# First modulation tiles regrouped by chunk, with the first norm's chunks finished pair by pair

## The chip, the cores and the metric

The kernel runs on one core of a Trainium2 chip. The metric is the device time of one execution in microseconds (us); lower is better. PE is TensorE (matrix multiply), PEld its weight loads, DVE is VectorE, ACT is ScalarE, POOL is GpSimd, SP is the engine whose queue issues most DMAs.

## The reference, cut to what matters

Two layers of a hybrid block (retention, neighbourhood attention and grouped attention, gated and merged) run on 256 latent and 256 context tokens of width 1024, followed by feed-forward and mixer stages. All is float32. At the head stands an adaptive norm; for layer 0:

```python
shift_x, scale_x, gate_x = jnp.split((c_silu @ ada_w + ada_b)[:, None, :], 3, axis=-1)
shift_y, scale_y, gate_y = jnp.split(cc_silu @ ada_w + ada_b, 3, axis=-1)
hx = rms_norm(x, norm_w) * (1.0 + scale_x) + shift_x
hy = rms_norm(y, norm_w) * (1.0 + scale_y) + shift_y
... = split_cols(hx @ w_in)
```

`ada_w` is 1024 x 3072 per layer, so scale and shift of layer 0 take 2048 of its columns, 8 MB. Everything that comes after needs hx and hy.

## The kernel before, in words

Activations lie transposed: 8 chunks of 128 features on the partitions, 512 token columns (256 latent, 256 context). Weights come as tiles of 128 x 1024 floats (512 KB), in the order of `TILES`, through a ring of 6 buffers `raw` that SP's queue refills as PE releases them (L1140 to L1154). A float32 product is made of three matmuls on rounded halves: each weight tile is split by ACT (`w_hi`, L1361) and DVE (`w_lo`, L1641), each activation chunk into `h_hi` and `h_lo`; `three` (L2117) multiplies them (L2121 to L2123). A product has 8 chunks of three matmuls, 24 in all.

The order of work is a list of steps that `build_schedule` writes (L695); every engine walks through the same list and runs its own part of each step in that order, with semaphore waits. An engine that waits in one step does nothing of the later ones.

The head before: SP loads half of the tokens and then the weight tiles; ACT's queue loads the parameters, the other half of the tokens and the tables `con` (610 KB, L1321). The first 16 tiles are the modulation weights of layer 0: eight of scale, then eight of shift (`ADA_FIRST`). One tile holds 128 of the 1024 input rows and all 1024 columns of its section, so a section is known only when its eighth tile is in. PE multiplies each tile by silu(c) with 32 columns of the array and 512 moving columns (L2168, two strips of 32 a tile; neighbouring tiles use the other two strips). After a section ACT copies the bank to `merge_tanh` (L1348), PE turns it (L2182), DVE adds the bias (L1681, L1683). Beside this ACT squares the tokens (L1371), DVE sums (L1654), PE takes means (`norm_mean`, L2211), DVE adds epsilon (L1714), POOL takes the power (L1220), PE spreads it (L2220) and DVE copies it to `rstd` (L1706). When scale is known DVE computes `m` = x * a * rstd for all chunks (L1668, 16 instructions of 256 columns). When shift is known ACT writes `h_hi` = m + shift (L1399) and DVE `h_lo` = m + shift - h_hi (L1777), chunk by chunk, with three weight splits between (at chunks 0, 3 and 6), and PE starts the first product. POOL loads and completes two bias tables beside it (L1176, L1181). Layer 1's norm (L1664, L1396, L1405, L1772) has the same work in another form: DVE x * rstd in one instruction, ACT scale and shift in place and a copy to `h_hi`, DVE the difference.

Of the kernel before, what the change touches and what calls it, by code (L numbers as in the profile page):

```python
# [54 lines left out]
ADA_FIRST = [(0, 1), (0, 0)]  # L55
# [5 lines left out]
def tile_order():  # L61

    out = [("ada", layer, section, k) for layer, section in ADA_FIRST for k in range(KC)]
# [120 lines left out]
def lay_out_params(a):  # L184
# [24 lines left out]
def shape_tables():  # L209
# [16 lines left out]

        "window": np.where((kc >= start) & (kc < start + 16), 0.0, -1e30),
# [49 lines left out]
class Schedule:  # L277


    def __init__(self):  # L280
# [4 lines left out]
        self.split_n = AHEAD  # L285
# [33 lines left out]
    def split_ahead(self, t):  # L319

        done = t - sum(tile[0] == "ada" for tile in TILES[:t])
# [34 lines left out]
    def product(self, what, src, n, blocks=KC, parts=(3, 3, 2), **fields):  # L356
# [10 lines left out]
        at = 0  # L367
        for part in (parts if blocks == KC else (2, 2)):
# [245 lines left out]
def ada_tile(s, section, k):  # L614
# [3 lines left out]
    if section not in ADA_FIRST:  # L618
        s.flush()
        s.split_ahead(s.tile)  # L620
# [60 lines left out]
def normed(s, norm, k):  # L681
# [3 lines left out]
    if split:  # L685
        st.at = s.count("shift") if norm.layer else None
# [8 lines left out]
def build_schedule():  # L695
# [4 lines left out]
    for k in range(KC):  # L700
        ada_tile(s, ADA_FIRST[0], k)
        if k == 3:
            norm_mean(s, norm)
        if k == 5:
            norm_spread(s, norm)
    for k in range(KC):
        ada_tile(s, ADA_FIRST[1], k)
        if k == 1:
            s.turn_due()
            s.add("ada_scale", layer=0)  # L710
            for i in range(KC):
                prescale(s, norm, i)
    s.turn_due()
    for layer in range(DEPTH):
        norm.how, norm.layer = "ada", layer
        if layer:
            s.add("ada_scale", layer=layer)
            rms(s, norm)
        for k in range(KC):
            if layer:  # L720
                for i in range(3 * k if k < 1 else k + 2, min(k + 3, KC)):
                    prescale(s, norm, i)
            elif k in (0, 3, 6):
                s.add("split", t=SPLIT_TILES[(0, 3, 6).index(k)])
            normed(s, norm, k)
# [125 lines left out]
def block_kernel(nc, weights, params, consts, tokens, rpb, gate_a, gate_x, spatial, spatial_b, out):  # L851
# [4 lines left out]
    with ctx:  # L856
# [44 lines left out]

        o_hi = {"a": hb("oa_hi", [P, 4, BOTH], F32R)}
# [25 lines left out]

        hb("reserved", [P, 8 * BOTH + 4 * BOTH + 2 * BOTH + BOTH + 4 * BOTH + 12 * P])
        half_tanh, head_sq = scaled[:, 0, :], scaled[:, 1, :]  # L930
        merge_tanh = hb("merge_tanh", [P, 2, BOTH])

        ada_rows = [merge_tanh[:, 0, :], bias[:, :, :, :].rearrange("p a b c -> p (a b c)")[:, 0:BOTH]]
        work = hb("work", [P, 4, BOTH])
        probs, probs_t = work[:, 0:2, :], work[:, 2:4, :]
        abs_dif = hb("abs_dif", [P, 3 * P])
# [57 lines left out]
        con_landed = sem("con_landed")  # L994
        tok_landed = [sem(f"tok_landed{i}") for i in range(4)]
        c_zero = sem("c_zero")
        ada_part = sem("ada_part")
        prescaled = sem("prescaled")
        shifted = sem("shifted")
# [89 lines left out]
        def rows_of(u):  # L1089
            return ada_rows[0 if (u.layer, u.c) in ADA_FIRST + [ADA_LAST] else 1]  # L1090

        def adds_on_dve(st):
            return st.norm.n == 0

# [41 lines left out]
        shift_turn = {st.u.layer: st.u for st in steps if st.kind == "ada_turn" and st.u.c == 0}  # L1136
# [26 lines left out]
        def _(pool):  # L1163
# [6 lines left out]
            def bias_step(st):  # L1170
# [3 lines left out]
                if reader[slot] is not None:  # L1174
                    pool.wait_ge(biased, reader[slot] + 1)
                pool.dma_start(bias[:, slot, :, :], rpb[g.layer, g.c]).then_inc(bias_landed[slot], 16)  # L1176
# [1310 lines left out]
```

## Time and profile before

| | us |
|---|---|
| median of 3 runs | 2096.53 (2094.64 to 2099.82) |
| the profiled execution | 2094.94 |
| its span, first to last instruction | 2093.0 |
| PE busy | 1993.6 (95%) |
| DVE busy | 1116.9 (53%) |
| ACT busy | 894.7 (43%) |
| POOL busy | 257.8 (12%) |

The span is cut into 40 slices of 52.3 us in the page; the whole head that the change touches lies in the first. In a timeline a row gives the start, the length, the engine, the line, what is written and read, how many instructions are merged, and in brackets the idle time before and what ended it.

### The profile page before, as it was taken

Reading aid. Unit: us, or ns where it says so; the run is one execution under the profiler, and the core shown is the slowest. Engines: PE = TensorE matmul, PEld = TensorE weight load, DVE = VectorE, ACT = ScalarE, POOL = GpSimd, SP = SyncE. Lnnn points to the kernel's source line nnn. Section 1 sums busy time; section 2 is a strip of 40 time slices with the busy share of each in tenths; the row PEclk is TensorE's granted clock in tenths of the full one; section 3 lists DMA queues with packets and bytes.
Section 4 is the critical chain, followed back from the end, with each engine's and each line's share of the span. In section 5 each row is a group of like instructions: output and inputs, shape, how many; then the busy total and the mean of one; then the engine's idle time right before and its main releaser. Section 6 shows DMA issues by size and latency. Waiting matters only on the chain.

```text
span 2093.0 us, 36804 instructions
## 1 busy us (share of the span) xinstructions
PE 1993.6 (95%) x13960; PEld 1782.5 (85%) x13960; DVE 1116.9 (53%) x1776; ACT 894.7 (43%) x1441; POOL 257.8 (12%) x278
## 2 busy tenths in 40 slices
PE   6999999999999999999989999899999999899998
PEld 3777777777786788888989998889999999899997
DVE  5454442455433664545565556865555555575554
ACT  4444231344332544335444444654444444554443
POOL 1000110110112101101131001400001000200001
PEclk9999999999999899999989999989999999899998
DMA  7221444311225223333445554445555555345552
GB/s 301 78 69 61 141 141 137 115 61 61 77 94 169 88 97 95 108 132 101 141 136 177 182 184 144 143 129 183 181 184 166 181 183 186 123 142 180 181 182 89
DMA packets 78970, 289.06 MB, mean 138 GB/s; under 512 B 8848, under 2 KB 8976, under 8 KB 78864
## 3 DMA queue, kind: packets, MB, share of 16 engines
q1 hardware_dynamic: 77168, 281.05, 40.6%
q0 software_dynamic: 1120, 4.72, 0.7%
q8 instruction: 76, 1.25, 0.2%
q10 hardware_dynamic: 576, 1.80, 0.2%
q14 instruction: 30, 0.25, 0.1%
HBM read 286.49 MB, written 1.05 MB: 137 GB/s over the span
## 4 chain that ended last, share of the span: by engine, by line
PE 59%; DVE 4%; issue 2%; ACT 2%; POOL 1%; POOLq 0%; DVEq 0%; ACTq 0%
PE bank L2121 18%; PE bank L2123 18%; PE bank L2122 18%; PE bank L2211 1%; ACT w_hi L1361 1%; PE bank L2290 1%; PE bank L2273 1%; DVE w_lo L1641 1%; PE bank L2259 1%; DVE h_lo L1721 1%; PE bank L2220 0%; PE bank L2330 0%; DVE x L2020 0%; DVE r_conv L2054 0%; PE bank L2315 0%
## 5 line engine op out<-in xcount | busy, mean ns | idle before, releaser
L2121 PE MATMUL bank<-h_hi,w_hi 128*128 128x256 f32 (+1 forms) x2720 | 874.5, 322 | 30.6 <-DVE h_lo L1721 12.6
L2123 PE MATMUL bank<-h_hi,w_lo 128*128 128x256 f32 (+1 forms) x2720 | 851.2, 313 | 0.0
L2122 PE MATMUL bank<-h_lo,w_hi 128*128 128x256 f32 (+1 forms) x2720 | 850.2, 313 | 0.0
L1641 DVE TENSOR_TENSOR w_lo<-raw,w_hi 128x1024 fp32r<-128x1024 f32 x484 | 597.2, 1236 | 415.8 <-ACT w_hi L1361 415.1
L1361 ACT ACTIVATE w_hi<-raw 128x1024 fp32r<-128x1024 f32 x484 | 509.8, 1055 | 524.9 <-PE bank L2123 467.1
L2121 PEld LDWEIGHTS bank<-h_hi,w_hi 128*128 128x128 f32 x2720 | 522.8, 192 | 93.8 <-issue 52.3
L2123 PEld LDWEIGHTS bank<-h_hi,w_lo 128*128 128x128 f32 x2720 | 522.9, 192 | 28.8
L2122 PEld LDWEIGHTS bank<-h_lo,w_hi 128*128 128x128 f32 x2720 | 523.9, 193 | 23.0
L2121 PE MATMUL bank<-hid_hi,w_hi 128*128 128x256 f32 x704 | 197.8, 281 | 1.8 <-DVE hid_lo L1982 1.8
L2123 PE MATMUL bank<-hid_hi,w_lo 128*128 128x256 f32 x704 | 197.6, 281 | 0.0
L2122 PE MATMUL bank<-hid_lo,w_hi 128*128 128x256 f32 x704 | 197.2, 280 | 0.0
L1255 POOL TENSOR_TENSOR silu_g<-silu_g,rstd 128x256 f32<-128x256 f32 x88 | 65.3, 743 | 659.3 <-ACT silu_g L1520 659.3
L2121 PEld LDWEIGHTS bank<-hid_hi,w_hi 128*128 128x128 f32 x704 | 132.9, 189 | 2.4 <-DVE w_lo L1641 2.4
L2122 PEld LDWEIGHTS bank<-hid_lo,w_hi 128*128 128x128 f32 x704 | 132.8, 189 | 0.0
L2123 PEld LDWEIGHTS bank<-hid_hi,w_lo 128*128 128x128 f32 x704 | 132.4, 188 | 0.0
L1520 ACT ACTIVATE silu_g<-silu_g 128x256 f32<-128x256 f32 x88 | 36.8, 418 | 163.0 <-DVE silu_g L1967 163.0
L1976 DVE TENSOR_TENSOR hidden<-silu_g,bank 128x256 f32<-128x256 f32 x88 | 37.0, 421 | 129.0 <-POOL silu_g L1255 126.5
L1458 ACT ACTIVATE work<-bank,row_stat 128x512 f32<-128x512 f32 (+1 forms) x96 | 58.3, 612 | 68.3 <-DVE row_stat L1862 68.3
L1468 ACT ACTIVATE work<-bank 128x512 f32<-128x512 f32 (+1 forms) x96 | 45.3, 525 | 78.8 <-PE bank L2273 78.6
L1862 DVE TENSOR_REDUCE row_stat<-bank 128x1 f32<-128x512 f32 (+1 forms) x96 | 53.1, 594 | 33.7 <-PE bank L2259 33.5
L1242 POOL TENSOR_TENSOR scaled<-scaled,square 128x512 f32<-128x512 f32 (+1 forms) x32 | 44.1, 1378 | 184.5 <-ACT square L1371 183.9
L1215 POOL TENSOR_TENSOR m<-m,square 128x512 f32<-128x512 f32 (+1 forms) x32 | 33.3, 1043 | 218.8 <-DVE square L1808 218.8
(223 smaller groups left out, 2142.1 us busy)
## 6 DMA issues: line engine op xcount, KB each, us to landing
raw<-in_weights SPq DMA_DIRECT2D x532, 512.0 KB, 3.3
bias<-in_rpb POOLq DMA_DIRECT2D x8, 384.0 KB, 3.6
x<-in_tokens SPq DMA_DIRECT2D x2, 512.0 KB, 6.1
x<-in_tokens ACTq DMA_DIRECT2D x2, 512.0 KB, 8.5
out<-rows_out SPq DMA_DIRECT2D x1, 1024.0 KB, 4.0
con<-in_consts ACTq DMA_DIRECT2D x1, 609.5 KB, 11.8
ws<-in_spatial POOLq DMA_DIRECT2D x1, 512.0 KB, 4.9
ws_b<-in_spatial_b POOLq DMA_DIRECT2D x1, 512.0 KB, 5.6
```

The source lines that it names most:

```text
L1242: pool.tensor_tensor(sum_sq[:, 0:n], sum_sq[:, 0:n], square_of(st), ALU.add).then_inc(sq_added, 1)
L1255: pool.tensor_tensor(v, v, rstd[:, 0:SEQ], ALU.mult).then_inc(silu_scaled, 1)
L1361: nc.scalar.activation(w_hi[:, n % SPLIT, :], raw[:, t % RAW, :], ACT.Copy).then_inc(hi_ready, 1)
L1458: nc.scalar.activation(probs[:, hp, 0:u.keys], S[use % 2][:, 0:u.keys], ACT.Exp, bias=row_stat[:, 0, i:i + 1], accum_out=row_stat[:, 1, i: ...
L1468: nc.scalar.activation(probs_t[:, hp, 0:u.keys], T[use % 2][:, 0:u.keys], ACT.Copy)\
L1520: nc.scalar.activation(silu_g[:, i % 2, :], silu_g[:, i % 2, :], ACT.Silu).then_inc(silu_ready, 1)
L1641: dve.tensor_tensor(w_lo[:, t % RAW, :], raw[:, t % RAW, :], w_hi[:, SPLIT_NO[t] % SPLIT, :].bitcast(F32), ALU.subtract).then_inc(lo_ready, 1)
L1862: dve.tensor_reduce(row_stat[:, 0, i:i + 1], s[:, 0:u.keys], AX_X, ALU.max, negate=True)\
L1976: dve.tensor_tensor(hidden[:, i % 2, :], silu_g[:, i % 2, :], S[i % 2][:, 0:SEQ], ALU.mult)\
L2121: nc.tensor.matmul(dst, w_hi[:, SPLIT_NO[t] % SPLIT, at], hi, start=start, stop=False, skip_group_check=shared)
L2122: nc.tensor.matmul(dst, w_hi[:, SPLIT_NO[t] % SPLIT, at], lo, start=False, stop=False, skip_group_check=shared)
L2123: return nc.tensor.matmul(dst, w_lo[:, t % RAW, at], hi, start=False, stop=stop, skip_group_check=shared)
```

## The change: what it does

- The 16 first tiles leave the ring and come from an array of their own, `first`: tile 2k is the shift columns and 2k+1 the scale columns of chunk k, with all 1024 rows. They land in buffers that are used only later (`early`, `early_o`, `work`), so none of them waits for another. SP issues all 16, with the first weight tile after pair 4, then five ring tiles, then the rest of the tables; ACT's queue loads only the first 133 table columns.
- For each pair PE makes 16 multiplications of 128 columns over four strips, ACT copies 256 columns, PE sums the strips with `parts` (two calls of two moving columns each), DVE adds the bias and makes `ada_a`. PE waits for ACT's copy inside the step.
- The first norm is done as in layer 1: x * rstd in one instruction (chunks 0 to 3 on DVE, 4 to 7 on POOL), then per chunk: even ones ACT (scale and shift in place, then a copy), odd ones ACT straight into `h_hi` and DVE the full value into `scaled`; DVE the difference.
- Steps now run: pairs 0 to 2, mean, pair 3, spread, the eight x * rstd, chunks 0 to 3, pair 4, chunk 4, pair 5, chunk 5, first weight split, pair 6, chunk 6, first two chunks of the first product, pair 7, chunk 7, three more splits, the rest of the product. POOL's first bias load waits for pair 7 to have landed.

```diff
-ADA_FIRST = [(0, 1), (0, 0)]
+def lay_out_first(a):
+    tiles = [column_tile(a["ada_w"][0], slice(D * c + P * k, D * c + P * k + P)) for k in range(KC) for c in range(2)]
+    return np.stack(tiles)
...
-CONSTS = [("ident", P), ("swap", P), ("cos", SEQ), ("sin", SEQ),
-          ("dif", 3 * P), ("window", GRID_W), ("ones", 1),
-          ("heads", 2)]
+CONSTS = [("ident", P), ("ones", 1), ("heads", 2), ("parts", 2),
+          ("swap", P), ("cos", SEQ), ("sin", SEQ), ("dif", 3 * P), ("window", GRID_W)]
+EARLY = P + 5
...
+        if self.hold:
+            parts = (2, 3, 3)
...
+    for k in range(KC - 1):
+        pair(k)
+        if k == 2:
+            norm_mean(s, norm)
         if k == 3:
-            norm_mean(s, norm)
-        if k == 5:
             norm_spread(s, norm)
...
             for i in range(KC):
                 prescale(s, norm, i)
-    s.turn_due()
+            for i in range(k + 1):
+                normed(s, norm, i)
+        if k > 3:
+            normed(s, norm, k)
+        if k == 5:
+            s.add("split", t=SPLIT_TILES[0])
+
+    def last_pair():
+        pair(KC - 1)
+        normed(s, norm, KC - 1)
+        s.hold = False
+        s.split_ahead(0)
+
+    s.background = [last_pair]
...
-            for t in range(RAW):
+            for k in range(KC):
+                for c in range(2):
+                    sp.dma_start(first_tiles[2 * k + c], first[2 * k + c, :, :]).then_inc(first_landed[k], 16)
+                if k == 4:
+                    sp.dma_start(raw[:, 0, :], weights[0, :, :]).then_inc(raw_landed[0], 16)
+            for t in range(1, RAW):
                 sp.dma_start(raw[:, t, :], weights[t, :, :]).then_inc(raw_landed[t], 16)
+            sp.dma_start(con[:, EARLY:], consts[:, EARLY:]).then_inc(tab_landed, 16)
...
+            def prescale_step(st):
+
+                if st.norm.layer or st.k < 4:
+                    return
+                pool.wait_ge(m_free, st.norm.m_spread + 1)
+                pool.tensor_tensor(m[:, st.k, :], x[:, st.k, :], rstd[:, :], ALU.mult).then_inc(pool_scaled, 1)
...
+            def ada_pair_step(st):
+
+                act.wait_ge(t_full, st.t_use + 1)
+                nc.scalar.activation(pair_rows[:, st.k % 2, :], T[st.t_use % 2][:, 0:SEQ], ACT.Copy)\
+                    .then_inc(t_free[st.t_use % 2], 1)
...
+                    ins = nc.scalar.activation((m if st.how == "act" else h_hi)[:, k, at], m[:, k, at], ACT.Identity,
+                                               bias=ada[:, norm.layer, k, j:j + 1], scale=ada_a[:, k, j:j + 1])
...
+            def ada_pair_step(st):
+
+                k = st.k
+                dve.wait_ge(m_full, st.m + 1)
...
+                dve.tensor_tensor(dst, M[:, 0:4].rearrange("p (c j) -> p c j", c=2), b, ALU.add).then_inc(m_free, 1)
+                dve.wait_ge(m_free, st.m + 1)
+                dve.scalar_tensor_tensor(out=ada_a[:, k, :], in0=ada[:, 0, KC + k, :], scalar=1.0,
+                                         in1=par[:, nw:nw + 1].to_broadcast([P, 2]), op0=ALU.add, op1=ALU.mult)\
+                    .then_inc(a_ready, 1)
...
+                if st.how == "dve":
+                    full = scaled[:, st.at % 2, :]
+                    dve.wait_ge(*scaled_by_norm(norm, k))
+                    dve.wait_ge(a_ready, k + 1)
+                    for j in range(2):
+                        at = slice(SEQ * j, SEQ * j + SEQ)
+                        ins = dve.tensor_scalar(full[:, at], m[:, k, at], ada_a[:, k, j:j + 1], ada[:, 0, k, j:j + 1],
+                                                ALU.mult, ALU.add)
+                    ins.then_inc(shift_dve, 1)
+                    dve.wait_ge(shift_dve, st.at + 1)
                 dve.wait_ge(h_hi_ready, st.h + 1)
+                dve.tensor_tensor(h_lo[:, k, :], full, h_hi[:, k, :].bitcast(F32), ALU.subtract)\
+                    .then_inc(h_lo_ready, 1)
...
+            def ada_pair_step(st):
+
+                k, use = st.k, st.t_use
+                if k == 0:
+                    pe.wait_ge(set_up_act, 2)
+                pe.wait_ge(first_landed[k], 32)
+                if use >= 2:
+                    pe.wait_ge(t_free[use % 2], use // 2)
+                for c in range(2):
+                    for i in range(KC):
+                        strip = 32 * (i % 4)
+                        ins = nc.tensor.matmul(T[use % 2][strip:strip + 32, P * c:P * c + P], c_silu[:, i, :],
+                                               first_tiles[2 * k + c][:, P * i:P * i + P], start=(i < 4), stop=(i >= 4),
+                                               skip_group_check=True)
+                ins.then_inc(t_full, 1)
...
+                pe.wait_ge(*t_out(use))
+                if st.m:
+                    pe.wait_ge(m_free, st.m)
+                for c in range(2):
+                    ins = nc.tensor.matmul(M[:, 2 * c:2 * c + 2], pair_rows[:, k % 2, P * c:P * c + P], C_("parts"),
+                                           start=True, stop=True)
+                ins.then_inc(m_full, 1)
```

## Rows read from the trace of the kernel before

**Rows 1.** Stages; columns: length, busy PE, PEld, DVE, ACT, POOL, PEclk, DMA, GB/s
```profile
11.00:17.30 6.30, 5.49 (x14) 0.78 (x16) 4.15 (x6) 3.67 (x6) 0.00 (x0) 1.00 1.02 411
...
37.80:44.60 6.80, 5.25 (x12) 4.12 (x13) 6.80 (x14) 6.80 (x15) 0.72 (x1) 0.50 0.39 155
```

**Rows 2.** Timeline of PE in the head, modulation tiles and norm
```profile
11.07 1.92 PE L2168 MATMUL bank<-raw,c_silu 128*32 128x512 f32 x4 [11.07 <-DMA raw<-in_weights]
...
19.72 1.07 PE L2168 MATMUL bank<-raw,c_silu 128*32 128x512 f32 x8
21.21 1.16 PE L2220 MATMUL bank<-con,stats 128*128 128x128 f32 x8 [0.42 <-POOL stats L1220]
...
32.80 1.05 PE L2168 MATMUL bank<-raw,c_silu 128*32 128x512 f32 x4 [0.24 <-DMA raw<-in_weights]
```

**Rows 3.** Timeline of all engines, from the squares to rstd
```profile
15.00 0.63 ACT L1371 ACTIVATE square<-x 128x512 f32<-128x512 f32 x1 [0.17 <-DVE scaled L1654]
...
17.84 0.38 PE L2211 MATMUL bank<-con,scaled 128*128 128x1 f32 x2
...
19.83 0.16 DVE L1714 TENSOR_SCALAR stats<-bank 128x4 f32<-128x4 f32 x1 [4.12 <-PE bank L2211]
20.14 1.02 POOL L1220 TENSOR_TENSOR stats<-stats,neg_half 128x4 f32<-128x4 f32 x1 [18.93 <-DVE stats L1714]
...
22.40 0.69 DVE L1706 COPY rstd<-bank 128x512 f32<-128x512 f32 x1 [2.42 <-PE bank L2220]
```

**Rows 4.** Timeline of all engines, from the last modulation tile to the first matmuls
```profile
34.64 0.65 PE L2182 MATMUL bank<-con,merge_tanh 128*128 128x128 f32 x4 [0.78 <-ACT merge_tanh L1348]
...
36.58 1.94 POOL L1181 TENSOR_TENSOR bias<-bias,con 128x768 f32<-128x768 f32 x1 [6.50 <-DMA bias<-in_rpb]
...
39.35 0.76 PE L2121 MATMUL bank<-h_hi,w_hi 128*128 128x512 f32 x1 [4.06 <-DVE h_lo L1777]
...
40.77 0.63 PE L2121 MATMUL bank<-h_hi,w_hi 128*128 128x512 f32 x1
...
42.05 0.63 PE L2121 MATMUL bank<-h_hi,w_hi 128*128 128x512 f32 x1
```

**Rows 5.** Timeline of PE, the first matmuls of the second product
```profile
47.87 0.39 PE L2121 MATMUL bank<-h_hi,w_hi 128*128 128x512 f32 x1
...
48.56 0.39 PE L2121 MATMUL bank<-h_hi,w_hi 128*128 128x512 f32 x1
```

**Rows 6.** One line each, min/median/max ns: L1777 around 37 us, then L1664
```profile
L1777 DVE SCALAR_TENSOR_TENSOR h_lo<-m,ada,h_hi x1: 2034/2034/2034, 36.8 to 36.8; 128x256 fp32r<-128x256 f32 x1
...
L1664 DVE TENSOR_TENSOR m<-x,rstd x8: 677/678/2300, 679.4 to 689.9; 128x512 f32<-128x512 f32 x8
```

**Rows 7.** Groups by shape, whole span: busy us, mean ns, idle before
```profile
L1641 DVE TENSOR_TENSOR w_lo<-raw,w_hi 128x1024 fp32r<-128x1024 f32 x484 | 597.2, 1236 | 415.8 <-ACT w_hi L1361 415.1
...
L1361 ACT ACTIVATE w_hi<-raw 128x1024 fp32r<-128x1024 f32 x484 | 509.8, 1055 | 524.9 <-PE bank L2123 467.1 <-DMA raw<-in_weights 57.4
...
L1215 POOL TENSOR_TENSOR m<-m,square 128x512 f32<-128x512 f32 x16 | 20.6, 1289 | 145.8 <-DVE square L1808 145.8
...
L1876 DVE TENSOR_SCALAR work<-work,row_stat 128x256 f32<-128x256 f32 x32 | 10.7, 376 | 0.0
...
L1399 ACT ACTIVATE h_hi<-m,ada 128x256 fp32r<-128x256 f32 x16 | 6.7, 494 | 0.3 <-DVE ada L1683 0.3
L1405 ACT ACTIVATE h_hi<-m 128x512 fp32r<-128x512 f32 x8 | 5.0, 630 | 0.3
...
L1598 ACT ACTIVATE sg_vt<-bank 128x256 f32<-128x256 f32 x8 | 3.0, 371 | 5.2 <-PE bank L2440 5.2
```

**Rows 8.** Timeline of ACT in layer 1's norm: scale and shift in place
```profile
683.48 1.08 ACT L1396 ACTIVATE m<-m,ada,ada_a 128x256 f32<-128x256 f32 x2
```

**Rows 9.** Timeline of PE, narrow matmuls on two strips of 64 columns
```profile
76.18 1.09 PE L2290 MATMUL bank<-work,v_s 128*64 128x128 f32 x16
```

More of the change, by code:

```diff
@@ L61, in tile_order @@
 def tile_order():
-    out = [("ada", layer, section, k) for layer, section in ADA_FIRST for k in range(KC)]
+    out = []
     for layer in range(DEPTH):
@@ L617, in ada_tile @@
         s.section = Step("section", s.count("section"), layer=section[0], c=section[1], t_use=s.use("T"))
-    if section not in ADA_FIRST:
-        s.flush()
-        s.split_ahead(s.tile)
+    s.flush()
+    s.split_ahead(s.tile)
     s.add("ada_tile", tile=s.tile, u=s.section, k=k)
@@ L685, in normed @@
     if split:
-        st.at = s.count("shift") if norm.layer else None
+        st.how = "act" if norm.layer or k % 2 == 0 else "dve"
+        st.at = s.count("shift_" + st.how)
     norm.chunks.append(st)
@@ L848, in ffn_tile, with block_kernel @@
     return (0 if i == 0 else 3 * i - 1) + (which == "u")
-def block_kernel(nc, weights, params, consts, tokens, rpb, gate_a, gate_x, spatial, spatial_b, out):
+def block_kernel(nc, weights, first, params, consts, tokens, rpb, gate_a, gate_x, spatial, spatial_b, out):
     schedule = build_schedule()
@@ L935, in block_kernel @@
         probs, probs_t = work[:, 0:2, :], work[:, 2:4, :]
+        first_tiles += [early_o[:, i, :] for i in range(4)]
+        first_tiles += [work[:, 2 * i:2 * i + 2, :].rearrange("p a b -> p (a b)") for i in range(2)]
         abs_dif = hb("abs_dif", [P, 3 * P])
@@ L994, in block_kernel @@
         con_landed = sem("con_landed")
+        tab_landed = sem("tab_landed")
+        first_landed = [sem(f"first_landed{i}") for i in range(KC)]
+        shift_dve = sem("shift_dve")
         tok_landed = [sem(f"tok_landed{i}") for i in range(4)]
@@ L1089, in rows_of, with scaled_by_norm @@
         def rows_of(u):
-            return ada_rows[0 if (u.layer, u.c) in ADA_FIRST + [ADA_LAST] else 1]
+            return ada_rows[0 if (u.layer, u.c) == ADA_LAST else 1]
         def adds_on_dve(st):
             return st.norm.n == 0
+        def scaled_by_norm(norm, k):
+            if norm.layer == 0 and k >= 4:
+                return pool_scaled, k - 3
+            return prescaled, 4 * norm.layer + k + 1
         def square_of(st):
@@ L1135, in block_kernel @@
         v_jobs = [st.job for st in steps if st.kind == "sg_v"]
-        shift_turn = {st.u.layer: st.u for st in steps if st.kind == "ada_turn" and st.u.c == 0}
+        layer_1_turn = {st.u.layer: st.u for st in steps if st.kind == "ada_turn" and st.u.c == 0}
         block = ctx.enter_context(nc.Block())
@@ L1767, in ada_normed @@
             def ada_normed(st):
-                k, layer = st.k, st.norm.layer
-                dve.wait_ge(h_hi_ready, st.h + 1)
-                if layer:
-                    dve.tensor_tensor(h_lo[:, k, :], m[:, k, :], h_hi[:, k, :].bitcast(F32), ALU.subtract)\
-                        .then_inc(h_lo_ready, 1)
-                    return
-                for j in range(2):
-                    at = slice(SEQ * j, SEQ * j + SEQ)
-                    ins = dve.scalar_tensor_tensor(out=h_lo[:, k, at], in0=m[:, k, at], scalar=ada[:, 0, k, j:j + 1],
-                                                   in1=h_hi[:, k, at].bitcast(F32), op0=ALU.add, op1=ALU.subtract)
-                ins.then_inc(h_lo_ready, 1)
+                norm, k = st.norm, st.k
+                full = m[:, k, :]
+                if st.how == "dve":
+                    full = scaled[:, st.at % 2, :]
[7 more added lines that the diff above has]
+                    dve.wait_ge(shift_dve, st.at + 1)
+                dve.wait_ge(h_hi_ready, st.h + 1)
+                dve.tensor_tensor(h_lo[:, k, :], full, h_hi[:, k, :].bitcast(F32), ALU.subtract)\
+                    .then_inc(h_lo_ready, 1)
             def value_turn_step(st):
@@ L2470 @@
         "weights": lay_out_weights(a),
+        "first": lay_out_first(a),
         "params": lay_out_params(a),
```

85 lines of the change are left out of this document (43 added, 42 removed).

## The prediction

> **What bounds the kernel now.** I read the head's stages first, since the change touches nothing behind the first product: 0.3% of this kernel, 6.3 us, is about what a measurement can tell from no change, so a head of some 48 us has to move by an eighth. In the stage from 11 to 17.3 us the DMA share is above 1 at 411 GB/s [rows 1]: a tile of 512 KB takes 1.28 us. The modulation tiles of before cost PE 1.05 us each and PE waits for the next one, to the last at 32.80 [rows 2]. So until then the head is bound by transfer. Behind the last tile stands a serial tail: copy and turn at 34.64, then DVE's first h_lo, which is caught behind POOL's bias addition (36.58, 1.94 us) and takes 2.03 us [rows 4, 6], so that the first matmul starts at 39.35 [rows 4]. From 37.8 to 44.6 the granted clock is 0.50, the lower level of 1.2 GHz, after PE had almost nothing to do [rows 1]: three matmuls of 512 columns take 1.28 us (40.77 to 42.05, 0.427 each) [rows 4], against 0.69 us (0.23 each) at 2.4 GHz [rows 5]. The second product starts at 47.87 [rows 5]. From there on PE has work without a break, so **the start of the second product is the mark**: the change is worth its shift. What could be gained is bounded too: with the last pair landing at 31.8 us the mark can hardly come before 38.
>
> **Transfers.** Before the last tile the change takes away the rest of the tables (about 0.55 MB by the sizes of the code, 1.35 us at 411 GB/s) and a bias load (0.39 MB, 0.96 us), and puts one weight tile (1.28 us): 32.80 - 1.35 - 0.96 + 1.28 = 31.8 us for pair 7. Pairs come every 2.55 us, with the weight tile behind pair 4: pair 0 at 12.7, pair 2 at 17.8, pair 3 at 20.3, pair 5 at 26.7, pair 6 at 29.2. SP's 17 issues come before the five ring tiles, which then land until about 39; no split asks for them earlier. The rest of the tables lands near 40, and only POOL's bias addition waits for it.
>
> **A pair on PE.** 16 calls make 32 matmuls of 128 columns, eight on each of four strips. Before, eight matmuls of 512 columns on four strips took 1.07 us [rows 2], two rounds of 0.43 in parallel. A quarter of the columns gives 0.107 a matmul, so 8 x 0.107 + 0.17 = 1.03 us if four strips run side by side, and 1.9 at half clock, as four matmuls on two strips took 1.92 at 11.07 [rows 2]. The other end: no overlap, 32 x 0.107 = 3.4 us. I take 1.03, since narrow matmuls do overlap: 16 on two strips took 1.09 us [rows 9]. The Trainium skill ("TensorE: Matmul & The Clock Gate", the part on 56 against 53.3 ns) says that with its hardware decode off PE spends about 62 ns on each matmul, which would make a pair 2.0 us. The mean of 0.068 us for 16 matmuls with the drain included [rows 9] leaves that open, and by it the mark would come some 3 us later. In the same step PE then waits for ACT's copy (0.37, as L1598) [rows 7] and sums the strips, four short matmuls like the four of the turn, 0.65 us [rows 4]. Pair 0 to pair 2 cannot overlap each other, since PE stands in the wait.
>
> **The norm comes later.** ACT is in its squares until 15.63 [rows 3], so pair 0's copy ends at 16.0 and PE is free at 17.0. Pair 1, clock still low: 1.9 + 0.4 + 0.6 to 19.9. Pair 2: 1.03 + 0.4 + 0.65 to 22.0. The mean takes 1.9 (17.84 to 19.83 less the wait) [rows 3] to 24.1, in place of 19.8. Pair 3 takes 2.1 to 26.3, the spread 1.16 [rows 2] to 27.7, the copy 0.69 [rows 3]: rstd is ready at 28.4, where it was at 23.1. POOL's power (1.02) [rows 3] hides beside pair 3. That is 5.3 us given away; before, it had a cover of ten microseconds (the shift tiles), and now everything behind it waits.
>
> **The chunks.** x * rstd is four times 0.68 on DVE [rows 6] and four times 1.29 on POOL [rows 7]. They don't run side by side: whenever POOL had a two-input operation running, DVE's stood, 2.03 us for a 0.47 us instruction and 2.30 for one of 0.68 [rows 6, 4]. Taking turns they need 4 x 0.60 (0.08 of an instruction overlaps the next) + 4 x 1.29 = 7.6, to 36.0. Without the collision it would be 2.4; with POOL's four in one piece the sum is the same for the last. Then DVE has four differences at 0.60 and two full values at two times 0.26 (two halves each of L1876's form, 0.38 less some 0.1 of overlap) [rows 7]: 3.5, to 39.8 with the drain. ACT (1.08 [rows 8] + 0.63 [rows 7] for an even chunk, 0.9 for an odd) keeps ahead. Only now does DVE come to pair 4's scale (0.35), to 40.1, though pair 4 had landed at 22.9: its step stands behind chunks 0 to 3. ACT 1.08 + 0.63 to 41.9, DVE 0.68. POOL's bias addition of 1.94 [rows 4] falls here (issued at 36, landed about 41; before, its DMA had ended the idle time in front of the addition too) and holds that difference up, so chunk 4 ends at 43.9. Pair 5: 0.35, ACT 0.9 to 45.2; then the weight split, 1.05 and 1.24 [rows 7], to 47.4. **The first product starts at 47.5**, 8 us later than now.
>
> **The product.** PE has been nearly idle since 28.7, so I take the low clock, as the clock fell before [rows 1]: six matmuls x 0.427 = 2.6, to 50.0. Pair 7 stands in the way with 1.9 + 0.4 + 0.65, to 53.0. By then I take the clock as back; 18 x 0.23 = 4.1 more, to 57.1. Chunk 7 (0.35 + 0.9 + 0.68) and the splits of tiles 1 and 2 are done beside it. The mark moves from 47.9 to 57.1, **9.2 us later**. The profiled execution takes 2094.94, so 2104.1; the median of the runs shown is 1.6 above it, 2096.53, and the prediction is 2105.7.
>
> Small terms at zero: the ring of 516 instead of 532 tiles, layer 1's norm (same instructions), the tables' order. Their cover is PE's own work; DMA has slack in every later slice, and if that were gone a tile would cost 1.28 us.
>
> **Bounds.** Low: the clock high throughout (0.9 for pair 1, 1.2 for six matmuls, 1.2 for pair 7) and a milder collision (a third of 5.1): mark near 52. High: strips not side by side (+3 to +4), the clock low until the end of the product (18 x 0.2 = 3.6): mark near 62.
>
> **Rivals.** (1) *The overlap works, faster.* If norm and chunks kept pace with the pairs, so that DVE has chunk 5 done when pair 6 lands, the first product would start near 31, pair 7's chunk would be ready at 31.8 + 1.03 + 0.4 + 0.65 + 0.35 + 0.9 + 0.68 = 35.8, and the mark would be at 38 to 42: 2088.6. It is decided at the copy of rstd: it would have to come by about 22. For it: the transfers leave room. Against: the three steps with a wait inside and ACT's squares until 15.63 [rows 3]. 0.06. (2) *No collision and a high clock, about equal.* DVE and POOL side by side take 5.1 off the chunks, of which pair 4 and ACT give back one; the low-clock terms go (3.3): mark at 49 to 51, 2098.6. Against it stand three long DVE instructions. With mixtures of it (mark under 54.2) 0.22. (3) *The clock never rises in the head.* Each pair costs 1.9 and the mean 3.3, rstd comes at 33.6, the mark at 61 to 64: 2111. PE's work on a pair is half of the time at most, which speaks for it; that its matmuls had the high level by 19.72 (8 in 1.07 us against 4 in 1.92 at 11.07, though the stage's PEclk reads 1.00 there too) with little more work before speaks against [rows 1, 2]. 0.12. (4) *The change doesn't do what it says*: chunks finished while later pairs land. I count this in the forecast: only if the first h_lo comes before 31.8 does it. My forecast, mark at 54.2 to 60: 0.60.
>
> **Numbers.** Faster by over 0.3% is rival 1, 0.06; within 0.3% is rival 2, 0.22; slower is the forecast and rival 3, 0.72. The range from 2098 (mark 49.4) to 2112 (mark 63.3) leaves out rival 1 and the tails of the others; the forecast alone would have 2102 to 2109.
>
> **What would show it.** In the profile after: pairs' matmuls 1.0 to 1.9 us long and the next pair's not before DVE's copy; rstd copied near 28; DVE instructions of over 1.5 us beside POOL's x * rstd; PE idle from about 29 to 47 but for pairs 4 to 6, waiting for ACT's and DVE's steps and not for DMA; the second product's first matmul near 57. I am wrong if rstd is ready by 24, if DVE's multiplications stay at 0.68 beside POOL, or if the first product starts before 40.

## The result, and the profile after

| | before | after |
|---|---|---|
| median of 6 runs, us | 2098.78 (2094.64 to 2100.17) | 2110.88 (2105.71 to 2113.07) |
| the profiled execution, us | 2094.94 | 2110.73 |
| its span, us | 2093.0 | 2108.5 |
| rstd copied (end) | 23.1 | 33.7 |
| first product starts | 39.35 | 51.78 |
| second product starts (the mark) | 47.87 | 61.74 |
| span behind the mark | 2045.1 | 2046.8 |

The ratio of after to before is **1.0059**, 95% interval [1.0044, 1.0074]: the change costs 12.1 us between the medians. The forecast was 2105.7 with a range of 2098 to 2112; the mark moved by 13.9 us where 9.2 were forecast. Before's profiled execution is 3.8 us below its median here, so the two traces lie further apart (15.5 us) than the medians. Of the 15.5 us between the two spans 13.9 lie before the mark and 1.7 behind it.

The stages of the head of after (columns as in [rows 1]), and below them two stretches far behind it:

```profile
11.00:17.30 6.30, 3.67 (x52) 3.20 (x56) 3.65 (x7) 3.39 (x6) 0.00 (x0) 1.00 1.03 412
17.30:40.00 22.70, 15.35 (x156) 12.75 (x148) 8.07 (x13) 6.04 (x12) 7.22 (x5) 1.00 0.96 384
40.00:51.70 11.70, 6.67 (x76) 5.49 (x76) 8.94 (x17) 5.15 (x11) 4.07 (x5) 1.00 0.24 69
51.70:56.90 5.20, 4.87 (x39) 3.21 (x39) 2.00 (x4) 1.98 (x4) 1.44 (x1) 1.00 0.01 2
56.90:61.70 4.80, 4.62 (x22) 3.92 (x23) 3.20 (x7) 3.65 (x6) 0.00 (x0) 1.00 0.02 3
...
385.00:388.00 3.00, 3.00 (x8) 2.34 (x7) 0.00 (x0) 1.06 (x1) 0.00 (x0) 0.50 0.63 246
446.00:449.40 3.40, 3.40 (x16) 2.65 (x15) 0.89 (x3) 1.93 (x5) 0.00 (x0) 0.51 0.00 0
```

The transfers came much as forecast (share of 0.96 or more to 40 us). PEclk needs care: the first change of clock on record in this trace is at 56.9 us, and the column prints 1.00 for all that lies before it, though the lengths of the matmuls there are those of the low level (a_warm below has a pair of the same 1.94 us where the clock on record is 0.50). The first of [rows 1] has the same gap: before's first change on record is at 17.3.

The 1.7 us behind the mark fit the clock. Behind 65 us the low level holds for 109.4 us in after and 106.2 in before; the 3.2 us more, at half speed, are some 1.6 us. The last two rows are low stretches that before lacks (it has none between 44.6 and 676 us); others differ both ways. The two rows are no mark of the change: b_split, a version of the kernel before (further down), has the same two.

```profile
374.90:378.20 3.30, 3.30 (x9) 2.59 (x8) 0.44 (x1) 0.82 (x1) 0.00 (x0) 0.50 0.56 201
436.30:439.60 3.30, 3.30 (x14) 2.40 (x12) 1.37 (x6) 2.02 (x6) 0.00 (x0) 0.50 0.00 0
```

PE, DVE and ACT of after, from the first pair to rstd (timeline; columns as in [rows 2]):

```profile
13.05 1.94 PE L2259 MATMUL bank<-early,c_silu 128*32 128x128 f32 x32 [13.05 <-DMA early<-in_first]
15.04 0.38 ACT L1399 ACTIVATE merge_tanh<-bank 128x256 f32<-128x256 f32 x1 [0.37 <-PE bank L2259]
15.57 0.99 PE L2269 MATMUL bank<-con,merge_tanh 128*128 128x2 f32 x4 [0.58 <-ACT merge_tanh L1399]
16.49 1.93 PE L2259 MATMUL bank<-early,c_silu 128*32 128x128 f32 x32
...
19.87 1.93 PE L2259 MATMUL bank<-early,c_silu 128*32 128x128 f32 x32
...
23.66 0.56 PE L2306 MATMUL bank<-con,scaled 128*128 128x1 f32 x2 [0.34 <-DVE ada L1734]
...
27.14 1.93 PE L2259 MATMUL bank<-early,c_silu 128*32 128x128 f32 x32
...
30.94 2.05 PE L2315 MATMUL bank<-con,stats 128*128 128x128 f32 x8 [0.35 <-DVE ada L1734]
32.92 1.94 PE L2259 MATMUL bank<-early,c_silu 128*32 128x128 f32 x32
33.02 0.69 DVE L1774 COPY rstd<-bank 128x512 f32<-128x512 f32 x1 [2.04 <-PE bank L2315]
```

All pairs take 1.93 or 1.94 us, pair 7 at 54.64 too. A step of PE is 1.93 + 0.5 (wait for ACT's copy) + 1.0 = 3.4 us, while pairs land every 2.55 (in a_warm, where PE waits for them, pair 0 starts at 12.81 and pair 2 at 17.93). The spread took 1.16 in before [rows 2] and takes 2.05 here; the means took 1.9 and take 3.5 (23.66 to 27.2). PE is the slow one in this stretch, with the clock at its lower level of 1.2 GHz.

From rstd to the first product:

```profile
33.75 5.71 DVE L1723 TENSOR_TENSOR m<-x,rstd 128x512 f32<-128x512 f32 x4
33.80 6.79 POOL L1277 TENSOR_TENSOR m<-x,rstd 128x512 f32<-128x512 f32 x4 [5.22 <-DVE rstd L1774]
...
39.38 1.75 DVE L1850 TENSOR_TENSOR h_lo<-m,h_hi 128x512 fp32r<-128x512 f32 x1
...
40.90 1.01 PE L2269 MATMUL bank<-con,merge_tanh 128*128 128x2 f32 x4 [6.05 <-ACT merge_tanh L1399]
41.85 1.93 PE L2259 MATMUL bank<-early_o,c_silu 128*32 128x128 f32 x32
...
44.85 1.09 ACT L1458 ACTIVATE m<-m,ada,ada_a 128x256 f32<-128x256 f32 x2 [4.00 <-DVE ada_a L1736]
...
46.51 0.37 ACT L1399 ACTIVATE merge_tanh<-bank 128x256 f32<-128x256 f32 x1
...
50.50 1.23 DVE L1701 TENSOR_TENSOR w_lo<-raw,w_hi 128x1024 fp32r<-128x1024 f32 x1 [0.18 <-ACT w_hi L1423]
...
51.78 0.79 PE L2193 MATMUL bank<-h_hi,w_hi 128*128 128x512 f32 x1
```

Here PE waits for the others. Pair 4 was multiplied by 34.9, but ACT's copy of it stands behind ACT's part of chunks 0 to 3, so PE idles 6.05 us in its step. DVE comes to pair 4's scale only behind its differences, so ACT idles 4.00 us, and pair 5, multiplied by 43.8, is copied at 46.51 because ACT first waits for pair 4's scale. PE to ACT to PE to DVE to ACT, each in its own fixed order.

### The profile page after: what moved, and what is told of

It reads as the page before. It is cut to its first block, busy times and chain, and to the rows that moved or that the text cites. A ratio compares the mean times of both kernels' runs of the same rounds, so it can differ in the third digit from the quotient of the medians.

```text
span 2108.5 us, 37245 instructions
## 1 busy us (share of the span) xinstructions
PE 2001.9 (95%) x14176; PEld 1799.1 (85%) x14176; DVE 1117.5 (53%) x1774; ACT 901.0 (43%) x1451; POOL 261.2 (12%) x282
## 4 chain that ended last, share of the span: by engine, by line
PE 58%; DVE 4%; issue 2%; ACT 2%; POOL 1%; POOLq 0%; DVEq 0%; ACTq 0%
PE bank L2193 18%; PE bank L2195 17%; PE bank L2194 17%; PE bank L2306 1%; ACT w_hi L1423 1%; PE bank L2385 1%; PE bank L2368 1%; DVE w_lo L1701 1%; PE bank L2354 1%; DVE h_lo L1789 1%; PE bank L2315 0%; PE bank L2425 0%; DVE x L2092 0%; DVE r_conv L2126 0%; ACT m L1458 0%
```

## The experiments

"Filler" below is an extra matmul on `c_silu` into a bank that nothing reads; its result is used nowhere. "Mark" is the start of the second product in the run's profiled execution. Ratios are to runs of the kernel before on the same chip.

### a_warm: PE's clock kept up

```diff
+            FILL = {0: (1, 128), 1: (1, 128), 2: (1, 128), 3: (1, 128), 4: (12, 256), 5: (6, 256), 6: (2, 256)}
...
                 if k == 0:
                     pe.wait_ge(set_up_act, 2)
+                    filler(8, SEQ)
...
                 ins.then_inc(t_full, 1)
+                filler(*FILL.get(k, (0, 0)))
```

> The changed kernel with idle PE time filled: 8 multiplications of 256 columns on silu(c) into an unused bank before pair 0, one of 128 columns after pairs 0 to 3, and 12, 6 and 2 of 256 columns after pairs 4, 5 and 6. If the low clock is the largest term (PE's steps before rstd at half speed, then six matmuls, pair 7 and its sum), rstd is copied near 26.5 in place of 33.0, the first product starts near 45 and the second near 53 to 54 (61.7 without the filling), so about 8 us less than the changed kernel, still 5 to 6 us over the kernel before. If instead the chain through DVE and POOL sets the end whatever PE's clock, the second product stays at 59 or later.

Ratio 1.0053 [1.0035, 1.0070]; rstd 31.8, first product 51.16, mark 60.40. Its stages (columns as in [rows 1]):

```profile
11.10:17.90 6.80, 4.96 (x80) 3.64 (x78) 3.62 (x8) 3.47 (x7) 0.00 (x0) 1.00 1.03 412
17.90:35.00 17.10, 16.38 (x137) 14.08 (x138) 4.84 (x10) 3.19 (x7) 4.15 (x3) 0.50 1.03 410
35.00:52.00 17.00, 12.59 (x116) 10.28 (x116) 13.93 (x21) 8.15 (x17) 8.07 (x7) 1.00 0.36 133
```

and three of its pairs in the timeline of PE (pairs 0, 2 and 5), with pair 4's scale on DVE:

```profile
12.81 1.08 PE L2268 MATMUL bank<-early,c_silu 128*32 128x128 f32 x32 [0.86 <-DMA early<-in_first]
...
17.93 1.94 PE L2268 MATMUL bank<-early,c_silu 128*32 128x128 f32 x32 [0.23 <-DMA early<-in_first]
...
39.60 1.08 PE L2268 MATMUL bank<-early_o,c_silu 128*32 128x128 f32 x32
...
42.68 1.32 DVE L1736 SCALAR_TENSOR_TENSOR ada_a<-ada,par 128x2 f32<-128x2 f32 x1
```

A pair takes 1.08 us at the high level and 1.94 at the low one, so the clock is what stretches it. But it could not be held by a warm start: it fell at 17.9, after a stretch in which PE was busy for 4.96 of 6.80 us with the end of the first filler, pairs 0 and 1, their sums and two small fillers, and stayed low to 35.0 although PE was busy for 16.38 of 17.10. And where the filler did hold it, from 35 to 52 us, the head gained nothing: behind rstd 19.4 us went by to the first product, against 18.1 in after. (The long filler in pair 4's step, 6.5 us, hides in its wait: the sum behind it starts 7.4 us behind rstd at 39.16, against 7.2 in after.) What was lost there is POOL's: its first bias addition (42.33, 1.65 us) fell on pair 4's scale, which took 1.32 us in place of 0.16. Without that 1.2 us the way would be some 18.2, by this sum, as in after. So the clock explains the part up to rstd, and hardly any of the part behind it. The clock fell once more, from 52.0 to 55.4, under the product.

### a_dve: no x * rstd on POOL

```diff
-            if norm.layer == 0 and k >= 4:
-                return pool_scaled, k - 3
-            return prescaled, 4 * norm.layer + k + 1
+            return prescaled, KC * norm.layer + k + 1
```

and the same split taken out of the steps of POOL and DVE; DVE does all eight.

> The changed kernel with all eight x * rstd on DVE and none on POOL. If the collision of DVE with POOL costs its full 5 us, the first product starts near 47 and the second near 57. If DVE is the bound in that stretch with or without POOL (eight at 0.60 are 4.8 us, against 6.8 us for the two taking turns), only 1 to 2 us come off chunk 0, and part of that is lost again behind the next steps: second product at 60 to 62.

Ratio 1.0048 [1.0031, 1.0066]; rstd 33.5, first product 51.71, mark 61.03. Timeline of a_dve, DVE and POOL:

```profile
33.57 4.90 DVE L1718 TENSOR_TENSOR m<-x,rstd 128x512 f32<-128x512 f32 x8
...
41.66 1.54 POOL L1228 TENSOR_TENSOR bias<-bias,con 128x768 f32<-128x768 f32 x1 [7.68 <-DMA con<-in_consts]
41.73 2.02 DVE L1845 TENSOR_TENSOR h_lo<-scaled,h_hi 128x512 fp32r<-128x512 f32 x1
```

Eight on DVE alone take 4.90 us; four on DVE and four on POOL were done only 6.8 us after they began. The collision is real (1.9 us), but little of it arrives: POOL, free earlier, added its bias at 41.66 in place of 45.95, and there it stretched a difference of 0.69 to 2.02, which takes 1.3 us back. Pair 4's scale came 0.7 us earlier. Then the second addition (46.70) stretched pair 5's scale from 0.16 to 0.83, and the first product came 0.07 earlier. So the run shows that taking x * rstd off POOL gains nothing in this order, and not that the collisions with POOL cost nothing.

### a_mean: the norm before the pairs

```diff
-        if k == 2:
+        if k == 0:
             norm_mean(s, norm)
-        if k == 3:
+        if k == 1:
             norm_spread(s, norm)
             for i in range(KC):
                 prescale(s, norm, i)
+        if k == 3:
```

> The changed kernel with the mean after pair 0 and the spread and the eight x * rstd after pair 1; chunks 0 to 3 still after pair 3. If the late norm is a term of its own (rstd at 33.7 where it could be at 26.7), the first product starts near 46 and the second at 55 to 57, 5 to 6 us less than the changed kernel. If the chain behind pair 3 (chunks 0 to 3 in front of pair 4's bias on DVE) is the bound whatever the norm does, under 2 us.

Ratio 1.0037 [1.0025, 1.0048]; rstd 26.8, first product 46.57, mark 56.45. Moving two steps past two pairs each brings rstd 7.0 us forward (two steps of PE at 3.4 us), of which 5.3 reach the mark, as expected. Most of the rest goes to POOL's first bias addition: at 41.57 it falls on pair 5's scale, which takes 1.39 us. The lateness of the norm, which the prediction named as given away, is a term of its own.

### a_lag: chunks two pairs behind, all on DVE

```diff
+    pair(0)
+    norm_mean(s, norm)
+    pair(1)
+    norm_spread(s, norm)
+    prescale(s, norm, 0)
+    prescale(s, norm, 1)
+    for k in range(2, KC - 1):
         pair(k)
...
+        normed(s, norm, k - 2) if k < 5 else None
+        if k < 5:
+            prescale(s, norm, 2 * k - 2)
+            prescale(s, norm, 2 * k - 1)
+        if k == 4:
+            normed(s, norm, 3)
...
+        if k >= 5:
+            normed(s, norm, k - 1)
```

> The changed kernel with another order of steps and POOL's x * rstd on DVE: pair 0, mean, pair 1, spread, then two x * rstd ahead of each pair and each chunk two pairs behind its own pair, so that no engine's copy or bias of a pair stands behind the chunks of earlier ones. If the round trips of PE, ACT and DVE through queues in order are what fills the 18 us from rstd to the first product, the first product starts at 41 to 44 with the low clock in the pairs (35 with the high one) and the second at 50 to 53, 4 to 6 us less than with the earlier norm alone. If the amount of work on DVE and ACT sets it, the first product stays near 46.

Ratio 1.0020 [1.0007, 1.0032]; rstd 26.8, first product 41.13, mark 51.53. With rstd where a_mean had it, the first product came 5.4 us earlier, and the way from rstd to it fell from 19.8 to 14.3 us. How much of these 5.5 us is the order of steps alone is not separated. Up to 1.9 can be x * rstd without POOL (a_dve's 4.90 against 6.8), and 1.2 is the bias addition, which held pair 5's scale up in a_mean and starts at 41.71 here, behind the first product. At least 2.4 are left for the order. Now the chunks do keep pace, and PE sets it. Pairs 3 to 6 in its timeline, the first one at the high level,

```profile
28.96 1.08 PE L2259 MATMUL bank<-early,c_silu 128*32 128x128 f32 x32
...
31.08 1.93 PE L2259 MATMUL bank<-early,c_silu 128*32 128x128 f32 x32
...
34.44 1.93 PE L2259 MATMUL bank<-early_o,c_silu 128*32 128x128 f32 x32
...
37.82 1.93 PE L2259 MATMUL bank<-early_o,c_silu 128*32 128x128 f32 x32
```

stand 2.1, 3.4 and 3.4 us apart, with hardly a gap. The version is still behind before.

### c_pipe and c_fill: two ways to shorten PE's step in a_lag

c_pipe cuts the step in two, so that PE multiplies a pair before it sums the last one:

```diff
+    def pair_sum(k):
+        st = s.add("ada_sum", k=k, t_use=uses[k])
+        st.m = s.use("M")
...
     pair(1)
+    pair_sum(0)
...
         pair(k)
+        pair_sum(k - 1)
```

> a_lag with the pair's step cut in two: PE multiplies pair k+1 before it sums the strips of pair k, so that it never stands waiting for ACT's copy (order: pair 0, means, pair 1, sum 0, spread, pair 2, sum 1, ...). Nothing is added or left out. Theory (PE's occupation per pair is the pace): at the low clock a pair is then 1.93 + 1.0 = 2.95 us instead of 3.4, and the mean no longer waits for a sum: rstd is copied near 25, the seventh pair ends about 3 us earlier than in a_lag, second product at 48.5 to 50.5. Rival (the chain through DVE and ACT sets the pace): each sum now comes a pair later, the chunks with it, and the second product stays at 51 to 52.5.

c_fill leaves the order and keeps PE's clock up:

```diff
                 if k == 0:
                     pe.wait_ge(set_up_act, 2)
+                    filler(8)
...
                 ins.then_inc(t_full, 1)
+                filler(3)
```

with 256 columns each, on the full array.

> a_lag with wide filler matmuls (256 columns, full array, result unused): eight before pair 0 and three in every pair's step, between the 32 matmuls and the wait for ACT's copy. Theory (what still keeps a_lag 3.7 us behind before is that a pair takes PE 3.4 us at the low clock, 1.93 + 0.5 + 1.0, while pairs land every 2.55 us; at the high clock it takes 1.08 + 0.9 + 0.61 = 2.6): the filler keeps the clock high from pair 1 or 2 on as it did in a_warm from 35 us, pairs are 1.08 us, rstd is copied by 24 to 25, the first product starts at 36 to 38 and the second at 45 to 47, the time level with before or 1 to 2 us below it. Rival (the chain through DVE and ACT sets the pace, PE's clock only stretches waits): the marks come within 1.5 us of a_lag's (first product 41.1, second 51.5). Second rival (filler in the step costs what it saves, since narrow matmuls drop the clock anyway): low clock stays, every step is 1 us or so longer, second product at 54 or later.

| | rstd | first product | mark | ratio |
|---|---|---|---|---|
| a_lag | 26.8 | 41.13 | 51.53 | 1.0020 [1.0007, 1.0032] |
| c_pipe | 24.5 | 38.09 | 52.04 | 1.0018 [1.0002, 1.0033] |
| c_fill | 24.6 | 37.90 | 47.01 | 0.9993 [0.9978, 1.0007] |

The timeline of c_pipe, pairs 4 and 5, a matmul of the first product, and DVE's splits behind chunk 7, the first of them tile 1's:

```profile
29.32 1.93 PE L2268 MATMUL bank<-early,c_silu 128*32 128x128 f32 x32
31.18 1.01 PE L2282 MATMUL bank<-con,merge_tanh 128*128 128x2 f32 x4
32.12 1.93 PE L2268 MATMUL bank<-early_o,c_silu 128*32 128x128 f32 x32
...
50.29 0.63 PE L2202 MATMUL bank<-h_hi,w_hi 128*128 128x512 f32 x1
...
50.56 4.63 DVE L1712 TENSOR_TENSOR w_lo<-raw,w_hi 128x1024 fp32r<-128x1024 f32 x4 [0.19 <-ACT w_hi L1434]
```

and the stages of c_fill, from the timeline's 18.5 us on (columns as in [rows 1]):

```profile
18.50:21.90 3.40, 3.40 (x24) 2.46 (x13) 0.00 (x0) 0.38 (x1) 0.74 (x1) 0.51 1.02 405
22.00:37.90 15.90, 15.55 (x221) 13.56 (x222) 12.70 (x29) 10.52 (x21) 0.78 (x1) 1.00 1.03 409
37.90:47.00 9.10, 8.67 (x68) 6.68 (x67) 6.14 (x14) 5.34 (x9) 2.04 (x2) 1.00 0.35 122
```

and its timeline at the end of the first product:

```profile
42.61 0.94 DVE L1736 SCALAR_TENSOR_TENSOR ada_a<-ada,par 128x2 f32<-128x2 f32 x1
...
45.73 4.86 DVE L1703 TENSOR_TENSOR w_lo<-raw,w_hi 128x1024 fp32r<-128x1024 f32 x3 [0.19 <-ACT w_hi L1425]
...
47.01 0.50 PE L2193 MATMUL bank<-h_hi,w_hi 128*128 128x512 f32 x1 [0.44 <-DVE w_lo L1703]
```

In c_pipe pairs are 2.8 us apart, and rstd and the first product come 2.3 and 3.0 us earlier: PE's occupation was the pace up to there. Then it is all given back: its product takes 13.95 us (38.09 to 52.04) where a_lag's took 10.4. Two things end it within 0.3 us of each other. The low level lasts to 51.1, so that 20 of its 24 matmuls and pair 7 run at half speed; and DVE has the split of tile 1, which the second product needs, only at 51.8, behind chunk 7, whose scale POOL's second addition stretched to 1.49 us. So a higher clock behind pair 7's sum (45.2) would not by itself have brought the mark forward by more than 0.3. The mark is in the rival's 51 to 52.5, though the first product contradicts the rival.

In c_fill the clock is low once, from 18.5 to 21.9, and high from 22.0 on; pairs take 1.08 us and the mark is at 47.01, at the end of what was expected: it is the first form of the change that is level with before. It differs from a_lag in the filler alone, so what kept a_lag 4.5 us behind it was the clock. But the form that the change needs then, another order and 32 useless matmuls, brings it to zero, and not to a gain. What ends c_fill's first product is no longer PE: the second one waits 0.44 us for DVE's first split in the rows above, which stands behind chunk 7. Pair 7's sum is made at 41.88, its scale takes 0.94 us beside POOL's addition, ACT and DVE finish chunk 7 at 45.5, and the split at 47.0. In a_lag PE waits for the same split (0.17 us) at 51.53.

### The other side: what the kernel before had to give

b_warm puts eight fillers of 256 columns behind the second turn of before, b_tables loads the tables' rest (0.55 MB) and the first bias table behind the last chunk, b_split moves the second and third weight split behind chunk 7, b_both is these last two together, and c_both is b_both with b_warm's filler.

```diff
+                if u.n == 1:
+                    for _ in range(8):
+                        nc.tensor.matmul(S[0][:, 0:SEQ], flat[:, 0:P], flat, start=True, stop=True)
```

```diff
+                if g.n == 0:
+                    pool.wait_ge(h_lo_ready, KC)
+                    pool.dma_start(con[:, EARLY:], consts[:, EARLY:]).then_inc(tab_landed, 16)
                 pool.dma_start(bias[:, slot, :, :], rpb[g.layer, g.c]).then_inc(bias_landed[slot], 16)
```

```diff
-            elif k in (0, 3, 6):
-                s.add("split", t=SPLIT_TILES[(0, 3, 6).index(k)])
+            elif k == 0:
+                s.add("split", t=SPLIT_TILES[0])
             normed(s, norm, k)
+            if layer == 0 and k == KC - 1:
+                s.add("split", t=SPLIT_TILES[1])
+                s.add("split", t=SPLIT_TILES[2])
```

> The kernel before with 8 multiplications of 256 columns behind the turn of the shift section, so that PE is busy from 35.3 to 38.7. If PE's idle time is what takes the clock down from 37.8 to 44.6, it stays up and the 12 slow matmuls cost 0.2 us less each: the second product starts at 45.4 in place of 47.9 and the time is 2.4 us less. If not, no change.

> The kernel before with its order, but the late part of the tables and the bias loads issued only when the chunks are done. 0.95 MB less stand in front of the last modulation tile (2.3 us at 411 GB/s) and no POOL addition holds DVE at chunk 0 (1.5 us). The last tile lands near 30.5, the first product starts at 35.5 to 36.5 in place of 39.4, the second at 44 to 45, 3 to 4 us less than before. If the transfer time isn't what the last tile waits for, only the 1.5 us.

> The kernel before with the weight splits of tiles 1 and 2 behind chunk 7 in place of at chunks 3 and 6. If the first product is bound by DVE's h_lo (as its unchanged 8.5 us at the high clock says), two splits of 1.2 us leave its path and the second product starts near 45.7, 2 us less. If PE's own clock is the bound, no change in the product's length.

> Both edits to the kernel before: second product at 42 to 43 in place of 47.9, time 5 us less (0.25%), if the two add up.

> b_both (late tables, splits 1 and 2 behind chunk 7) with b_warm's eight filler matmuls of 256 columns behind the turn of shift (result unused). In b_both the first 13 matmuls of the first product took 0.43 us each (35.59 to 41.27) and the others 0.23, while DVE's differences took 0.81 us a chunk, so there the clock, which did not matter in b_warm, should matter. Theory: PE is idle from 33.1 to 35.6 in b_both and the filler takes 8 x 0.26 = 2.1 us of it at the high clock; the clock then stays high and the product is bound by the chunks at 0.81 us each, second product at 41.8 to 42.8 in place of 43.9, the time 1 to 2 us lower. Rival (the filler runs at the low clock and holds the first product up, as b_warm's did by 1.8 us): first product at 37 or later, second product at 43.5 or later, no gain.

The last modulation tile comes at a somewhat different time in each execution, so the table gives the way from it to the mark as well:

| | last tile | first product | mark | tile to mark | ratio |
|---|---|---|---|---|---|
| before | 32.80 | 39.35 | 47.87 | 15.1 | |
| b_warm | 34.86 | 41.16 | 49.68 | 14.8 | 1.0004 [0.9989, 1.0019] |
| b_tables | 32.00 | 37.04 | 45.68 | 13.7 | 0.9973 [0.9961, 0.9985] |
| b_split | 37.35 | 42.35 | 49.63 | 12.3 | 0.9985 [0.9976, 0.9995] |
| b_both | 30.59 | 35.59 | 43.91 | 13.3 | 0.9961 [0.9947, 0.9975] |
| c_both | 30.95 | 36.55 | 42.74 | 11.8 | 0.9968 [0.9954, 0.9983] |

b_warm's first product ran at the high level, with 0.39 where [rows 4] has 0.63, and took the same 8.52 us. (It starts 1.8 us later than before's because the last tile came 2.1 us later, and not by the filler, as the text on c_both above has it.) A row of its timeline, PE in the first product, shows what PE waits for:

```profile
44.57 0.51 PE L2121 MATMUL bank<-h_hi,w_hi 128*128 128x512 f32 x1 [0.96 <-DVE h_lo L1777]
```

In before the clock of 0.50 beside the first product, which the prediction read as a cost, cost nothing: DVE, with its differences and two splits in between, set that pace. With the splits moved away (b_both) DVE's eight chunks run in one piece and PE's clock becomes the limit; c_both shows the same product at the high level. Timelines of DVE and PE, first b_both:

```profile
34.56 6.46 DVE L1784 SCALAR_TENSOR_TENSOR h_lo<-m,ada,h_hi 128x256 fp32r<-128x256 f32 x16
...
36.15 0.63 PE L2129 MATMUL bank<-h_lo,w_hi 128*128 128x512 f32 x1
```

and c_both, with DVE's row the same and PE's shorter:

```profile
34.92 6.47 DVE L1784 SCALAR_TENSOR_TENSOR h_lo<-m,ada,h_hi 128x256 fp32r<-128x256 f32 x16
...
36.97 0.39 PE L2129 MATMUL bank<-h_lo,w_hi 128*128 128x512 f32 x1
```

The product takes 8.32 us in b_both and 6.19 in c_both. The mark comes 1.2 us earlier (PE waits 0.33 us for DVE's split there), and the two ratios are too near to tell these kernels apart, so the 1 to 2 us that c_both was to gain are not shown.

Of the other expectations, b_tables has the 1.5 us of POOL's addition (5.0 us from the last tile to the first product, 6.55 in before), but its last tile came only 0.8 earlier in place of 2.3, and its mark missed 44 to 45. b_split's gain from tile to mark is 2.8 us, near the 2 expected. b_both's mark came at 43.91, behind its 42 to 43: 13 of its matmuls are slow. **b_both beats both kernels**, by 0.39% [0.25%, 0.53%] against before (5 runs), with nothing of the change in it but the late tables, and no instruction of the computation more or less. Its 7 us between the medians are more than the 4.0 by which the mark moves in the two traces; before's trace is 3.3 us faster than the median of the runs that b_both is compared with, so the marks may understate it.

## Why the prediction was right, and where it was off

The result lies in the range and on the predicted side, 5.2 us above the forecast. Of that, 2.3 us are the kernel before itself, whose median is 2098.78 here and was 2096.53 for the forecast; the change costs 12.1 where 9.2 were forecast. The side was right for reasons that the traces bear out: the late norm, the steps in fixed order, the pairs' work on PE. But before rstd it was rival 3 that ran, which had a chance of 0.12 (rstd 33.6, mark 61 to 64, 2111 us; measured 33.7, 61.74, 2110.88). That its time agrees to a fraction of a microsecond is in part luck, since before's median moved and the span behind the mark grew. The range held because it was wide enough to take rival 3 in.

- **Transfers.** Pair 7 landed near 32.9 (there POOL's wait for it ends in a_lag), 31.8 forecast; behind pair 0 they bound nothing in after, as said. In c_fill, where PE keeps up, pair 6's matmuls start at 35.13 and don't wait for DMA.
- **A pair on PE.** Its size was right at either level: 1.03 and 1.9 forecast, 1.08 and 1.93 measured; the strips do run side by side. The Trainium skill ("TensorE: Matmul & The Clock Gate", the part on 56 against 53.3 ns) has about 62 ns for each matmul with hardware decode off, which would put 32 at 2.0 us, an estimate from that figure. By that rule a_warm's row is out of reach: 32 in 1.08 us is 34 ns each. So the 62 ns are not paid here; how the decode was set no run shows.
- **The clock is the step that failed.** The forecast took it as high from pair 2 on, because before's PE had it at 19.72 "with little more work before". The work was not little more: from 11 to 17.3 us before's PE was busy for 5.49 us [rows 1], after's for 3.67. The clock was low in all of after's head up to 56.9. The error runs up term by term: pairs 1 and 2 ended at 23.3 against 22.0, the means at 27.2 against 24.1, pair 3 at 30.6 against 26.3, rstd at 33.7 against 28.4. That is 5.3 us, and the whole of the miss on rstd; two waits of PE for DVE's bias, 0.34 and 0.35 us, are in it, and the rest is PE's work at half speed.
- **The chunks.** From rstd to the first product 19.1 us were forecast and 18.1 measured. The sum was right and one of its causes was not: the turn-taking of DVE and POOL was there (5.71 and 6.79 us side by side, 6.8 in all against 7.6), but taking it away moved the mark by 0.7 us where rival 2 had priced it at 4, since POOL's bias additions then took 2.0 us back. Behind it waits the same chain of round trips, which the forecast had in its sum as pair 4's scale and pair 5's; a_lag shows 5.5 us there, of which 2.4 at least are the order. POOL's bias addition took 1.54 beside a difference that grew from 0.69 to 1.40: 0.7 us where the sum has 1.3, and it held nothing up, since DVE then waited for PE. The second addition, which the forecast left out, took 2.17 at 50.97 and held pair 6's scale up by 1 us, beside the product.
- **The product.** 9.6 us forecast, 9.96 measured, with the low level up to and into pair 7's step.
- **The mark as the measure.** Right for the first product's side; behind it 1.7 us more were lost, about what 3.2 us more at the low level make. The prediction had put all that at zero.
- **Rival 1** (the overlap works) was decided where it was said, at rstd. c_fill is the nearest to it, with rstd at 24.6, 2.6 us behind the "by about 22", chunks in pace and a high clock. Its mark is 5 to 9 us behind rival 1's 38 to 42 and only draws level, which the later rstd alone doesn't account for: pair 7's own chain and the split of tile 1 behind it end at 47.0. A run with rstd at 22 there is not.
- **Reading of before.** The prediction put the low clock from 37.8 among before's costs, and so counted its return as something a change could gain. b_warm denies it.
- **Bounds.** The high end is added up wrongly: 57.1 and 3 to 4 and 3.6 make 64 to 65, not 62. The measured 61.74 lies inside either.

What stays open: whether c_fill would gain with pair 7 or the split of tile 1 at another place, and what POOL's bias additions cost it; how the 5.5 us from a_mean to a_lag divide between order and POOL; and what makes the clock's later low stretches differ between these traces.

## What to carry to other kernels

When a bulk step is cut into pieces so that later work can overlap it, count the round trips through in-order engines per piece, not the bytes: here eight pieces brought eight times a copy, a sum and a wait on PE, and put the rare but long-lead work (the norm) behind them. Put the long-lead chain first in every engine's order, and let the consumers lag a piece or two. And before a slow clock is counted as a cost, look at which engine ends the waits beside it.

## What was not expected of the hardware

- PE stayed at the lower level of its clock for the whole of a_warm's stretch from 17.9 to 35.0 us while it was busy for 16.38 of 17.10 us with narrow pairs, sums of two columns, means of one column and small fillers; in c_fill, with three fillers of 256 columns on the full array in each step, it was high from 22.0 on, after a low stretch from 18.5 to 21.9. In c_pipe, too, PE was busy for 24.36 of the 25.00 us from 13 to 38, and its pairs there took 1.93 us to the last.
- The Trainium skill ("SBUF — State Buffer", the part on who interferes with whom) says that of a DVE and a POOL instruction on their shared port the later one stands until the other ends. The traces agree: beside POOL's bias addition of 1.69 us a_lag's DVE (timeline below) took 1.97 us for two instructions that take 0.73 together elsewhere; the second, which began after POOL's, has 1.51 of it.

```profile
41.59 1.97 DVE L1845 TENSOR_SCALAR scaled<-m,ada_a,ada 128x256 f32<-128x256 f32 x2
...
41.71 1.69 POOL L1233 TENSOR_TENSOR bias<-bias,con 128x768 f32<-128x768 f32 x1 [8.05 <-DMA con<-in_consts]
```
